# An S5 scan whose states are stored by place in the block, and matmuls that take their columns 16 apart

## What is computed

```
def s5_scan(u, lam_re, lam_im, log_dt, b_re, b_im, c_re, c_im):
    lam_bar = jnp.exp(lam * dt)
    bu = jnp.einsum('blgc,gnc->blgn', u, b_bar)
    _, xs = lax.associative_scan(_scan_op, (lam_bar, bu), axis=1)
    return jnp.einsum('blgn,gcn->blgc', xs, c).real

y_f = s5_scan(ug, ...forward...)
y_b = s5_scan(ug[:, ::-1], ...backward...)[:, ::-1]
y = jax.nn.gelu(y_f + y_b + ssm_d * u)
```

## Time and profile before

| what | us |
|---|---|
| median of 3 runs | 2655.62 (2653.62 to 2661.03) |
| the profiled execution | 2654.97 |
| its span | 2653.2 |
| TensorE busy | 2535.5 |
| VectorE busy | 1713.0 |
| GpSimd busy | 1059.8 |
| ScalarE busy | 971.8 |
| mean granted TensorE clock | 0.986 of full |

### The profile page before, as it was taken

How to read it: one execution, slowest core, us unless ns; L and a number is a source line. 1 busy time by engine, 2 the same in 40 slices (tenths; PEclk the granted TensorE clock), 3 DMA queues, 4 the chain that set the end, 5 groups by cost and what they waited for, 6 DMA issues and landing times. The chain is left out here.

```text
span 2653.2 us, 34577 instructions
## 1 busy us (share of the span) xinstructions
PE 2535.5 (96%) x12222; PEld 2082.2 (78%) x12222; DVE 1713.0 (65%) x2253; ACT 971.8 (37%) x1770; POOL 1059.8 (40%) x1211
## 2 busy tenths in 40 slices
PE   7999988999998899999989999999999999999898
PEld 6887776788887588878868888877888887778786
DVE  5211765687896174544687677788767767674886
ACT  5221776512211250124353333343333334532432
POOL 2072534487882000012244454334344434443442
PEclk9999999999998899999999999999999999999999
DMA  6483988645429736455434222214322223455465
GB/s 215 136 292 109 183 165 221 209 146 166 136 96 220 173 135 230 174 152 167 139 90 153 88 88 88 72 51 125 103 88 88 72 82 137 171 192 205 149 208 183
DMA packets 322597, 390.99 MB, mean 147 GB/s; under 512 B 52352, under 2 KB 255104, under 8 KB 314368
## 3 DMA queue, kind: packets, MB, share of 16 engines
q1 hardware_dynamic: 276224, 310.65, 39.0%
q10 hardware_dynamic: 40384, 46.72, 5.4%
q0 software_dynamic: 5824, 31.46, 3.4%
HBM read 255.07 MB, written 133.69 MB: 147 GB/s over the span
## 5 line engine op out<-in xcount | busy, mean ns | idle before, releaser
L529 PE MATMUL tl_banks<-gu_b_hi,gu_a_hi 128*128 128x512 f32 x1848 | 726.0, 393 | 36.7 <-DVE gu_b_lo L1984 20.6
L531 PE MATMUL tl_banks<-gu_b_lo,gu_a_hi 128*128 128x512 f32 x1848 | 722.3, 391 | 0.0
L530 PE MATMUL tl_banks<-gu_b_hi,gu_a_lo 128*128 128x512 f32 x1848 | 722.2, 391 | 0.0
L529 PEld LDWEIGHTS tl_banks<-gu_b_hi,gu_a_hi 128*128 128x128 f32 x1848 | 348.7, 189 | 121.9 <-issue 34.8
L531 PEld LDWEIGHTS tl_banks<-gu_b_lo,gu_a_hi 128*128 128x128 f32 x1848 | 348.8, 189 | 73.4
L530 PEld LDWEIGHTS tl_banks<-gu_b_hi,gu_a_lo 128*128 128x128 f32 x1848 | 349.3, 189 | 71.3
L1978 DVE TENSOR_TENSOR gu_a_lo<-gu_raw,gu_a_hi 128x512 fp32r<-128x512 f32 (+1 forms) x340 | 293.7, 865 | 149.5 <-ACT gu_a_hi L1675 149.5
L1675 ACT ACTIVATE gu_a_hi<-gu_raw 128x512 fp32r<-128x512 f32 (+1 forms) x340 | 208.6, 616 | 349.3 <-PE tl_banks L531 295.3
L1350 POOL TENSOR_TENSOR gu_s_one<-gu_raw 128x512 f32<-128x512 f32 (+1 forms) x68 | 93.3, 1373 | 347.3 <-DVE gu_a_lo L1978 215.7
L1363 POOL TENSOR_TENSOR gu_raw<-gu_s_one,gu_raw 128x512 f32<-128x512 f32 (+1 forms) x68 | 97.8, 1439 | 162.2 <-DVE gu_a_lo L1978 161.8
L1675 ACT ACTIVATE gu_a_hi<-gu_s_one 128x512 fp32r<-128x512 f32 (+1 forms) x136 | 83.8, 616 | 148.6 <-PE tl_banks L531 121.5
(11 more groups left out here) (317 smaller groups left out, 5032.1 us busy)
## 6 DMA issues: line engine op xcount, KB each, us to landing
gu_raw<-in_w_ffn_gate SPq DMA_DIRECT2D x44, 512.0 KB, 3.8
gu_raw<-in_w_ffn_up SPq DMA_DIRECT2D x44, 512.0 KB, 3.7
gs_w_raw<-in_w_in SPq DMA_DIRECT2D x40, 512.0 KB, 4.5
gates<-gs_gate_out ACTq DMA_DIRECT2D x64, 256.0 KB, 2.9
br_rows<-gates POOLq DMA_DIRECT2D x16, 1024.0 KB, 7.1
gu_raw<-f SPq DMA_DIRECT2D x32, 512.0 KB, 4.0
dn_y<-down_sums SPq DMA_DIRECT2D x16, 1024.0 KB, 5.0
down_sums<-dn_y SPq DMA_DIRECT2D x15, 1024.0 KB, 6.0
```

Source lines behind the costliest of these rows:

```text
L529: pe.matmul(out, w_hi, x_hi, start=first, stop=False, skip_group_check=again)
L530: pe.matmul(out, w_lo, x_hi, start=False, stop=False, skip_group_check=again)
L531: return pe.matmul(out, w_hi, x_lo, start=False, stop=last, skip_group_check=again)
```

## The change

`states[d]` becomes `[128, 2, 16, 17, 16]`: rows by place, and in a row the 16 blocks next to each other. There are 16 rows for the places and one more, an edge row. In time order, chunk j*16 + i is now at row i, column j. What follows from it:

- The into products and `own_tokens` take `u`'s columns through `by_row`, so that the matmul's columns come out in the order (place, block): the 256 columns are read as 16 runs of 16 with a step of 16 elements.
- `lay_out` and the products out of the states read and write 16 whole rows, 256 contiguous elements. The neighbouring chunk is now the neighbouring row; for the first place (forward) or the last one (backward) it is the edge row. That row is filled by the new `put_edge`: one copy of the last places of 15 blocks, between `of_last` and `into_next`, in both scans. `STEPS` grows by one.
- The steps of the scan read and write rows: contiguous runs of 16 or 15 elements in the wide steps. `of_last` takes one element of a row.
- Gelu reads PSUM contiguously and writes `y` back in time order, with a step of 16 elements.
- `states` needs more memory (272 for 257 columns). The second `gate_out` slot moves to the end of `bases.memory`, `RING_U` goes from 8 to 6 groups and `MID_U` from 4 to 5, so that 21 groups and not 20 are loaded after the gates.

```diff
+def by_row(columns):
+    return columns.rearrange("p (j i) -> p i j", i=SCAN_I)
...
-    STEPS = 1 + ChunkScan.PER_STEP * (2 * SCAN_I + SCAN_J - 3)
-    RING_U, MID_U = 8, 4
+    STEPS = 2 + ChunkScan.PER_STEP * (2 * SCAN_I + SCAN_J - 3)
+    RING_U, MID_U = 6, 5
...
-    states = [m.sb(f"states{d}", [P, 2, QS, SSM_J + 1]) for d in range(2)]
+    states = [m.sb(f"states{d}", [P, 2, QS, SCAN_I + 1, SCAN_J]) for d in range(2)]
...
-    gate_out = m.sb("gate_out", [P, 2, BANK])
+    gate_out = [m.sb("gate_out", [P, BANK])[:], bases.memory[:, RING * D - BANK:RING * D]]
...
-                                 into[:, d, g // 2, g % 2].rearrange("p r n -> p (r n)"), u_whole[:, g, :],
+                                 into[:, d, g // 2, g % 2].rearrange("p r n -> p (r n)"), by_row(u_whole[:, g, :]),
...
-                pe.matmul(banks[:, n % 4 * 2 + e, 0:SSM_J], local[:, g // 8, g % 8, :], mine, start=True, stop=False)
+                pe.matmul(banks[:, n % 4 * 2 + e, 0:SSM_J], local[:, g // 8, g % 8, :], by_row(mine), start=True, stop=False)
...
-                                         states[d][half, r, q, d:d + SSM_J],
+                                         states[d][half, r, q, d:d + SCAN_I].rearrange("p i j -> p (i j)"),
...
-            copy(states[d][e * SSM_N:(e + 1) * SSM_N, r, q, 1 - d:1 - d + SSM_J],
+            copy(states[d][e * SSM_N:(e + 1) * SSM_N, r, q, 1 - d:1 - d + SCAN_I].rearrange("p i j -> p (i j)"),
...
-            act.activation(y[:, n // 2 % 2, q % 2 * 2:q % 2 * 2 + 2], banks[:, n % 4 * 2:n % 4 * 2 + 2, 0:SSM_J],
+            act.activation(y[:, n // 2 % 2, q % 2 * 2:q % 2 * 2 + 2].rearrange("p e (j i) -> p e i j", i=SCAN_I),
+                           banks[:, n % 4 * 2:n % 4 * 2 + 2, 0:SSM_J].rearrange("p e (i j) -> p e i j", i=SCAN_I),
...
+                if n == SCAN_I + SCAN_J - 2:
+                    scan.put_edge(dve)
...
-        self.grid = states[:, :, :, 1 - d:1 - d + SSM_J].rearrange("p r q (j i) -> p r q j i", i=SCAN_I)
+        self.grid = states[:, :, :, 1 - d:1 - d + SCAN_I]
...
-        target, source = (self.grid[:, :, :, :, bass.ds(n, 1)].rearrange("p r q j i -> p r q (j i)")
+        target, source = (self.grid[:, :, :, bass.ds(n, 1), :].rearrange("p r q i j -> p r q (i j)")
...
-        target = self.grid[:, :, :, targets, bass.ds(now, 1)].rearrange("p r q j i -> p r q (j i)")
-        return (target, self.grid[:, :, :, sources, self.end], bass.ds(i, 1), SCAN_J - 1,
+        target = self.grid[:, :, :, bass.ds(now, 1), targets].rearrange("p r q i j -> p r q (i j)")
+        return (target, self.grid[:, :, :, self.end, sources], bass.ds(i, 1), SCAN_J - 1,
...
+    def put_edge(self, engine):
+        engine.wait_ge(self.done, self.PER_STEP * (SCAN_I + SCAN_J - 2) + 1)
+        engine.tensor_copy(self.edge, self.ended).then_inc(self.done, 1)
```

More of the change, by code:

```diff
@@ L3299, in gates_and_states @@
     middle = first_mid // 2
-    u_last = bases.memory[:, RING_U * SSM_J:2 * RING_U * SSM_J].rearrange("p (g j) -> p g j", g=RING_U)
+    u_last = bases.memory[:, 8 * SSM_J:(8 + RING_U) * SSM_J].rearrange("p (g j) -> p g j", g=RING_U)
     u_mid = u_flat[:, 3 * size:3 * size + MID_U * SSM_J].rearrange("p (g j) -> p g j", g=MID_U)
@@ L3498, in _ @@
                 act.wait_ge(gate_stored[s], n // 2 * 16)
-            act.activation(gate_out[:, s], banks[:, 6 + s, :], ACT.Sigmoid).then_inc(gate_free, 1)
+            act.activation(gate_out[s], banks[:, 6 + s, :], ACT.Sigmoid).then_inc(gate_free, 1)
             act.wait_ge(gate_free, n + 1)
-            act.dma_start(gate_rows[b, :, c * BANK:(c + 1) * BANK], gate_out[:, s]).then_inc(gate_stored[s], 16)
+            act.dma_start(gate_rows[b, :, c * BANK:(c + 1) * BANK], gate_out[s]).then_inc(gate_stored[s], 16)
         load_chunks(act, u_rest, u_scratch, u_in, 1, u_parts)
@@ L3525, in scan_parts @@
         def scan_parts(scan):
-            for step in scan.steps():
+            for n, step in enumerate(scan.steps()):
+                if n == SCAN_I + SCAN_J - 2:
+                    scan.put_edge(dve)
                 for part in range(4):
@@ L3530, in scan_parts @@
                     yield
-        dve.memset(states[0][:, :, :, 0:1], 0.0).then_inc(edge_zero, 1)
-        dve.memset(states[1][:, :, :, SSM_J:SSM_J + 1], 0.0).then_inc(edge_zero, 1)
+        dve.memset(states[0][:, :, :, 0, 0:1], 0.0).then_inc(edge_zero, 1)
+        dve.memset(states[1][:, :, :, SCAN_I, SCAN_J - 1:SCAN_J], 0.0).then_inc(edge_zero, 1)
         for g in range(GROUPS):
@@ L3557, in __init__ @@
         self.d, self.on_pool, self.leaps = d, on_pool, leaps
-        self.grid = states[:, :, :, 1 - d:1 - d + SSM_J].rearrange("p r q (j i) -> p r q j i", i=SCAN_I)
+        self.grid = states[:, :, :, 1 - d:1 - d + SCAN_I]
         self.end = SCAN_I - 1 if d == 0 else 0
+        edge = states[:, :, :, 0 if d == 0 else SCAN_I]
+        ended = self.grid[:, :, :, self.end]
+        self.edge, self.ended = (edge[:, :, :, 1:], ended[:, :, :, :-1]) if d == 0 else (edge[:, :, :, :-1], ended[:, :, :, 1:])
         self.by_re, self.by_im = by_re, by_im
@@ L3576, in of_last @@
         now, last = (i + 1, i) if self.d == 0 else (SCAN_J - 2 - i, SCAN_J - 1 - i)
-        target, source = (self.grid[:, :, :, bass.ds(n, 1), self.end] for n in (now, last))
+        target, source = (self.grid[:, :, :, self.end, bass.ds(n, 1)] for n in (now, last))
         return target, source, slice(SCAN_I - 1, SCAN_I), 1, i * self.PER_STEP + (self.PER_STEP * (SCAN_I - 1) + 1)
@@ L3586, in into_next @@
             now = SCAN_I - 1 - i
-        target = self.grid[:, :, :, targets, bass.ds(now, 1)].rearrange("p r q j i -> p r q (j i)")
-        return (target, self.grid[:, :, :, sources, self.end], bass.ds(i, 1), SCAN_J - 1,
-                i * self.PER_STEP + (self.PER_STEP * (SCAN_I + SCAN_J - 2) + 1))
+        target = self.grid[:, :, :, bass.ds(now, 1), targets].rearrange("p r q i j -> p r q (i j)")
+        return (target, self.grid[:, :, :, self.end, sources], bass.ds(i, 1), SCAN_J - 1,
+                i * self.PER_STEP + (self.PER_STEP * (SCAN_I + SCAN_J - 2) + 2))
+    def put_edge(self, engine):
+        engine.wait_ge(self.done, self.PER_STEP * (SCAN_I + SCAN_J - 2) + 1)
+        engine.tensor_copy(self.edge, self.ended).then_inc(self.done, 1)
     def part(self, engine, step, n):
@@ L3628, in run @@
         self.over_blocks(engine)
+        self.put_edge(engine)
         with engine.Fori(0, SCAN_I - 1) as i:
```

## The result

| | before | after |
|---|---|---|
| median, runs of the same chip | 2654.62 (2651.41 to 2661.03) | 2683.65 (2680.19 to 2684.5) |
| span of the profiled execution | 2653.2 | 2678.4 |
| first product out of the states starts | 854.01 | 871.38 |
| last Gelu ends | 904.46 | 934.19 |

The ratio is 1.0114, 95% interval 1.0096 to 1.0131: 29 us slower, where 37 were forecast. The page's busy times (to the earlier trace rows): TensorE is busy 32 us longer, VectorE 75 and GpSimd 60 us less. The scans became as much cheaper as wanted, and the kernel slower.

What follows compares the result with a forecast made beforehand. The prediction took TensorE, busy 96% of the span, to bound the kernel. From 2654.97 us it summed +26.9 (products in), -3.3 (scans and last `u` loads), +12.9 (products out) and +0.5 (Gelu) to 2692 us, range 2645 to 2702.

Steps and rivals of the forecast that it cites:

- Products in: Products into the states: 128 instructions with stepped reads at 0.466 us each, 59.6 us against 32.7, +26.9.
- The scans: Wide scan steps become packed, saving 3.3 us on VectorE before `w_lo`; gate products end 6.05 us sooner.
- `w_lo`'s wait: TensorE's 3.94 us wait at 833 to 836.9 falls to 0.6 us and the clock stays up.
- The wait before the products out: TensorE's idle time until the last `u` loads land: about 6 us instead of 3.3, loads 3.3 us sooner.
- steps 2 and 3: Cheaper scans and last `u` loads together: -3.3 us, any gate gain beyond that given back in waiting.
- Products out with Gelu: Products out of the states, stepped reads of `u` +12.9 us, and Gelu's stepped write +0.5.
- steps 4 and 5: Products out: 64 instructions on `u` at 0.466 us each, +12.9; Gelu's stepped write, +0.5.
- Gelu: Stepped write takes 0.597 to about 1.11 us, 16 times; only the last shows, +0.5 us.
- `u`'s split: First `u_rest` group needed one pair (3 us) sooner; up to 2 us late only where TensorE isn't slowed.
- Case C: Rival: TensorE reads stepped columns as fast as packed; 2652 us, no measurable change; chance 0.27.
- Case D: Rival: stepped reads free and last `u` loads landing at 846.3, 7.7 us sooner; 2645 us; chance 0.13.

Runs made afterwards that it cites:

- experiment 2: Kernel before the change, with only TensorE's reads of `u` stepped 16 apart in both places (wrong column order): 2683.1 us, ratio 1.012.
- experiment 9: Kernel of experiment 5 with the last six groups of `u` loaded at 751 us, when GpSimd's own scan has ended: 2652.21 us, ratio 0.9999.
- experiment 5: Kernel after the change, with `u` written in row order by ScalarE's already stepped copy in project in, all reads packed: 2653.3 us, ratio 1.0002.
- experiment 1: Kernel after the change, with TensorE reading `u`'s columns packed in both places (wrong column order): 2650.4 us, ratio 1.0003.
- 4: Kernel after the change, with `u` read packed and TensorE writing its columns 16 apart into PSUM: 2650.83 us, ratio 1.0001.
- 6: Kernel of experiment 5 with the near-token table loads moved to GpSimd's queue, behind the fourth table: 2661.89 us, ratio 1.0038.
- 7: Kernel before the change, with only the near-token table loads moved to GpSimd's queue, behind the fourth table: 2660.86 us, ratio 1.0035.
- 12: Kernel before the change, with its last eight `u` groups and four more loaded earlier and the near-token tables in two parts: 2653.51 us, ratio 1.0004.

## Why the prediction was right

The sign, the place and the size were forecast. One more row of the kernel after is used below, from its products out, with the same columns as the windows above:

```profile
872.00:875.00 3.00, 3.00 (x9) 2.18 (x8) 0.00 (x0) 0.79 (x1) 0.00 (x0) 0.50 1.16 126
```

1. **Products in, +26.9 forecast, +22.2 measured** (54.93 against 32.71). The mechanism was right, the size too large: 0.429 us an instruction, 1.68 ns an element, where 1.82 had been read off VectorE and ScalarE. This mis-sized term is most of the miss of 8 us. That 1.82 came so near is in part luck. The reasoning was one fetch per element at the price of the memory, the same on every engine; but a `fp32r` instruction fetches 512 elements and pays 0.43 to 0.49 as well, 0.84 to 0.96 ns an element. Nor is it TensorE reading at half its own rate, as the step from 0.228 to 0.43 might suggest. Behind the wait, at a granted clock of 0.50 (the window above; 0.83 in the last of the five us), the first twelve products take 5.42 us to the next line's start with stepped reads (871.38 to 876.80), and before took 5.39 with packed ones (854.01 to 859.40); half of the rate there would be some 10 us. And at a clock of 1.00 the same twelve stepped products take 5.32 us (874.40 to 879.72 in experiment 2). So the stepped pace, 0.43 to 0.45 us, does not follow the clock, and at 1.2 GHz the step costs nothing.
2. **The scans.** 480 elements take 0.658 us (0.65 forecast), 240 take 0.407 (0.40). `put_edge` took 1.01 us on GpSimd and is hidden. `w_lo`'s wait was to be 0.6 us and is none, the clock stayed up: the gates are 7.0 us shorter (6.05 forecast).
3. **The wait before the products out**, about 6 us forecast, 5.38 measured; the net of steps 2 and 3 was to be -3.3 and is -4.9 (871.38 - 854.01 - 22.2, less 0.1 for the start). The size holds, and so does the object, but it was not the only one: the tables of `local`, which stood in the prediction as the cause that `u` comes late, land at the same moment as `u` (871.14). The time depends little on it, the remedy does: in experiment 9, with `u` out of the way, the tables still hold the start back to 846.93, 1.2 us sooner than in 5.
4. **Products out with Gelu, +13.4 forecast (steps 4 and 5), +12.4 measured** (62.8 against 50.4 from first product to last Gelu). The starts are 0.43 apart. Of it, 13 pairs at 0.84 us more are 10.9, the last Gelu is 0.4, and 1.1 is the wait at 887.53, which the sum did not have. The twelve products at the lower clock, 12 x 0.039 in the sum, cost nothing.
5. **Gelu** takes 1.02 to 1.04 us (1.11 forecast) and shows only at its end.
6. **`u`'s split**, up to 2 us late where TensorE isn't slowed: 3.3 us in experiment 1, 1.8 in 5. In the kernel after, where it was to cost nothing, it is the 1.1 us at 887.53: products out at 3.8 us a pair leave `u_rest` more time, but not enough.

22.2 - 4.9 + 12.4 = 29.7, the medians say 29.0. The two profiled spans differ by 25.2 only: the stages behind were 4.5 us shorter in the one of after, which lies within the spread of the runs (10 us before, 4 after). Case C (2652) is what came of experiments 1, 4 and 5: had TensorE's reads been free, the change would have been worth nothing, by the mechanism named there. Case D's 846.3 was not reached even with packed reads (847.49): the tables and the last `u` landed at 847.2 there, and the wait for `u_rest` came behind them.

What stays open: the rule behind TensorE's price. Free are, for float32, a step of 2 and runs of 2 and more, and two runs in turn are nearly so (0.27); for `fp32r` runs of 4 and more are free or nearly so (0.23 to 0.25), and a step of 2 or runs of 2 nearly double it. On this the Trainium skill, "SBUF — State Buffer", section "Specifications (TRN2)", wants at least two hits on a 16-byte line for full bandwidth. That TensorE pays at step 4 agrees. Runs of 2 in `fp32r`, two hits a line at half pace, don't, and neither does a pace that is much the same at one hit (0.43 to 0.49, steps 4 to 64) as at two (0.45, step 2).

## What to carry to other kernels

A layout that makes one engine's operands packed moves the step to another reader. Price it on the engine that bounds the kernel, and put the step where it is free (here TensorE's write into PSUM, or a copy that has a step already), or where that engine isn't waited for. When a stage ends sooner than its successor's loads, look at every load that the successor needs, in the order of need: here the tables and the last `u` came up together and `u_rest` behind them, and only when the last `u`, the tables and part of `u_rest` had all been moved did the gain appear. An earlier load is not free: three times here it came beside the weights and made them late (experiments 6, 7 and 12).

## What was not expected of the hardware

- A stepped write of 256 float32 columns into PSUM was free for TensorE (0.230 us an instruction), a stepped read of the same columns from SBUF was not (0.429).
- The same stepped read cost nothing at the lower clock: twelve products took 5.42 us stepped and 5.39 packed, both behind a wait and at a granted clock of 0.50 or little above. At 1.00 they took 5.32 stepped.
- Step 128 over 256 columns, two runs read in turn, was nearly free (0.27, packed 0.23), step 64 was not (0.44).
- The transfer engines were full at 175 GB/s from 843 to 863 in experiment 5 (the window below; share, then GB/s). From 800 to 848 of it single slices moved over 400. So bytes alone do not set the time; which property of these transfers (short rows, 16 partitions each) does it was not tried.

```profile
843.00:863.00 20.00, 13.23 (x70) 9.66 (x70) 0.00 (x0) 4.97 (x5) 0.00 (x0) 0.83 1.13 175
```
